# A sum over groups of heads, split by halves of the heads: one half beside the last attention, the other beside the output projection

## The reference

```python
    alpha = jax.nn.softmax(jnp.stack(lses, axis=0), axis=0)
    o = jnp.sum(alpha[..., None] * jnp.stack(outs, axis=0), axis=0)
    y = o.reshape(B, S, DIL_WIDTH).astype(h.dtype) * jax.nn.silu(gate)
    return y @ w_out
```

## Time and profile before

| what | value |
|---|---|
| median of 3 runs | 2482.21 us |
| lowest and highest run | 2479.74, 2485.02 us |
| the profiled execution's own time | 2479.8 us |
| its span in the trace | 2478.0 us |
| PE busy | 2193.9 us, 89% of the span |
| DVE, ACT, POOL busy | 953.9, 873.6, 865.2 us |

### The profile page before, as it was taken

The page is one execution under the profiler, slowest core; times in us unless marked ns, Lnnn a source line. Parts: engine busy times, 40 slices in busy tenths (PEclk is TensorE's granted clock), DMA queues, the critical chain, the costliest instruction groups (busy, mean ns, idle before and its releaser), DMA issues. The chain is left out here.

```text
span 2478.0 us, 26013 instructions
## 1 busy us (share of the span) xinstructions
PE 2193.9 (89%) x10048; PEld 1736.3 (70%) x10048; DVE 953.9 (38%) x1603; ACT 873.6 (35%) x1740; POOL 865.2 (35%) x454
## 2 busy tenths in 40 slices
PE   4998999999957997857999999887987998999998
PEld 3877788888846775646677777675765456887876
DVE  1333334633453356553253411247552642210121
ACT  2544445655353554323232122231322222321231
POOL 3422233333314322244344433342224313444442
PEclk9999999999978999978999999898998998999999
DMA  4312122222332211222352233232223432332321
GB/s 154 100 53 69 52 84 71 86 86 81 129 110 75 90 52 58 70 85 85 102 149 89 86 86 94 73 102 69 81 79 124 131 113 66 96 103 85 102 90 64
DMA packets 130634, 221.32 MB, mean 89 GB/s; under 512 B 8744, under 2 KB 58456, under 8 KB 130304
## 3 DMA queue, kind: packets, MB, share of 16 engines
q1 hardware_dynamic: 110720, 168.63, 22.5%
q0 software_dynamic: 9104, 32.66, 4.0%
q10 hardware_dynamic: 10688, 18.35, 2.1%
HBM read 199.40 MB, written 19.62 MB: 88 GB/s over the span
## 5 line engine op out<-in xcount | busy, mean ns | idle before, releaser
L2238 POOL TENSOR_TENSOR lo_ring<-raw_ring,hi_ring 128x1024 fp32r<-128x1024 f32 (+1 forms) x304 | 732.0, 2430 | 1188.3 <-ACT hi_ring L1891 1188.2
L855 PE MATMUL bank<-xh,hi_ring 128*128 128x512 f32 x1472 | 601.7, 409 | 5.4 <-DVE xl L1337 3.3
L855 PE MATMUL bank<-xh,lo_ring 128*128 128x512 f32 x1472 | 582.4, 396 | 0.0
L855 PE MATMUL bank<-xl,hi_ring 128*128 128x512 f32 x1472 | 581.6, 395 | 0.0
L1891 ACT CAST hi_ring<-raw_ring 128x1024 fp32r<-128x1024 f32 (+1 forms) x304 | 303.4, 1046 | 512.9 <-PE bank L855 491.2
L855 PEld LDWEIGHTS bank<-xh,hi_ring 128*128 128x128 f32 x1472 | 282.5, 192 | 77.2 <-issue 18.5
L855 PEld LDWEIGHTS bank<-xh,lo_ring 128*128 128x128 f32 x1472 | 281.0, 191 | 61.5
L855 PEld LDWEIGHTS bank<-xl,hi_ring 128*128 128x128 f32 x1472 | 282.5, 192 | 57.8 <-issue 2.6
L855 PE MATMUL bank<-hi_ring,xh 128*128 128x512 f32 (+1 forms) x608 | 249.8, 411 | 11.4 <-POOL lo_ring L2238 6.4
L855 PE MATMUL bank<-hi_ring,xl 128*128 128x512 f32 (+1 forms) x608 | 242.2, 398 | 0.0
L855 PE MATMUL bank<-lo_ring,xh 128*128 128x512 f32 (+1 forms) x608 | 242.2, 398 | 0.0
(11 more groups left out here) (246 smaller groups left out, 2477.7 us busy)
## 6 DMA issues: line engine op xcount, KB each, us to landing
raw_ring<-in_ffn_w_in SPq DMA_DIRECT2D x176, 256.0 KB, 3.1
raw_ring<-in_dil_w_in SPq DMA_DIRECT2D x80, 512.0 KB, 3.7
raw_ring<-in_ffn_w_out SPq DMA_DIRECT2D x44, 512.0 KB, 3.8
raw_ring<-in_diff_w_in SPq DMA_DIRECT2D x32, 512.0 KB, 3.7
raw_ring<-in_w_in SPq DMA_DIRECT2D x32, 512.0 KB, 3.7
arena<-scratch_heads POOLq DMA_DIRECT2D x4, 1584.0 KB, 13.9
scratch_gates<-arena ACTq DMA_DIRECT2D x24, 256.0 KB, 2.1
arena<-scratch_gates POOLq DMA_DIRECT2D x24, 256.0 KB, 3.8
```

Source lines behind the costliest of these rows:

```text
L855: ins = T.matmul(bank[pb][:, 0:S if p.form == "feature" else p.cols], lhsT, rhs, start=(k == 0 and m == 0), stop=(k == p.K - 1 and m == le ...
L2238: G.tensor_tensor(lo, raw_ring[:, p % RAW, 0:q.kq * q.n], hi.bitcast(F32), ALU.subtract).then_inc(lowered, 1)
```

## The change

The three groups are summed by halves of 8 heads. Half 0 (units 0, 2, 4) is done beside the gate panels, while unit 5's attention still runs: one job of it to a mac. For this unit 4's attention is placed more densely (`LAST_RATIO` 1.1), the first two tiles of half 0 are loaded by POOL ahead of the gate panels, and tiles 2 and 3 by ACT, once the tile that held their place is summed. Half 1 is loaded by POOL after unit 5's store. After the gate panels half 0 is turned (4 transposes a tile, one bank), rounded, and its four remainders are made before any work of half 1. The first output panel begins with the 4 chunks of half 0; its second step for tile n waits for the turned half 1 of tile n (`late`), and half 1's jobs stand between its macs. ACT now scales 12 of the 24 slices of a half tile (4 of group 1 and 8 of group 2), DVE 12. The barrier ahead of the output panels is gone; waits on `mixed` take its place where the outputs are written over the gate. The norm row has a place of its own and is loaded after unit 5's store.

```diff
-ACT_HEADS = 12
+SCALED = 4
+HALF_ROW = 8 * ROW
...
-UNIT_RATIO, GATE_RATIO, FIRST_HEADS = 0.85, 2.5, 14
+UNIT_RATIO, LAST_RATIO, GATE_RATIO = 0.85, 1.1, 2.5
...
-        interleave(projections(u), side, UNIT_RATIO)
+        interleave(projections(u), side, LAST_RATIO if u == 5 else UNIT_RATIO)
...
-    def first_heads():
-        plan.job("mix_load")
-        for _ in range(FIRST_HEADS):
+    def first_half():
+
+        for n in range(2):
+            plan.job("mix_load", 0, n)
+        for step in range(16):
             yield
-        plan.job("mix_ratio", 0)
-        plan.job("mix_weight", 0)
-        plan.job("mix_scale", 0)
-
-    interleave(gate_panels(plan, w, 9 * D, 0), chain(side, first_heads()), GATE_RATIO)
+            if step % 3 == 2 and step < 12:
+                plan.job("mix_ratio", 0, step // 3)
+            elif step % 3 == 0 and 0 < step < 13:
+                n = step // 3 - 1
+                plan.job("mix_weight", 0, n)
+                plan.job("mix_scale", 0, n)
+            elif step % 3 == 1 and 1 < step < 14:
+                n = step // 3 - 1
+                plan.job("mix_sum", 0, n)
+            if step in (9, 10, 13, 14):
+                plan.job("mix_gate", 0, (9, 10, 13, 14).index(step))
+
+    def last_store():
+        plan.job("row", "post0")
+        for n in range(NT):
+            plan.job("mix_load", 1, n)
+        yield
+
+    side, beside = chain(side, last_store()), first_half()
+    owed = 0.0
+    next(beside)
+    for _ in gate_panels(plan, w, 9 * D, 0):
+        owed += GATE_RATIO
+        while owed >= 1.0:
+            owed -= 1.0
+            next(side, None)
+        next(beside, None)
+    run_all(side)
+
+    use = [plan.job("mix_turn", 0, n, banks=(4 + n,)) for n in range(NT)]
     for n in range(NT):
+        plan.job("mix_lower", 0, n)
+    plan.job("mix_ratio", 1, 0)
+    plan.job("mix_weight", 1, 0)
+    plan.job("mix_scale", 1, 0)
+    plan.job("mix_ratio", 1, 1)
+    plan.job("mix_sum", 1, 0)
+    plan.job("mix_weight", 1, 1)
+    plan.parts = tuple(((f"drained{4 + n}", use[n][0]),) for n in range(NT))
+    late = [(), (), (), ()]
+    main = plan.panel("y", "dil_w_out", 0, 512, "tile", at=(0,), late=late)
+    for _ in range(4):
+        next(main)
+    for n in range(NT):
+        plan.job("mix_gate", 1, n)
+        use = plan.job("mix_turn", 1, n, banks=(4 + n,))
+        late[n] = ((f"drained{4 + n}", use[0]),)
         if n + 1 < NT:
-            plan.job("mix_ratio", n + 1)
-        plan.job("mix_sum", n)
-        if n + 1 < NT:
-            plan.job("mix_weight", n + 1)
-        plan.tile_parts("mix", n)
-        if n + 1 < NT:
-            plan.job("mix_scale", n + 1)
-        if n:
-            plan.job("lower", n - 1)
-    plan.job("lower", NT - 1)
+            plan.job("mix_scale", 1, n + 1)
+            if n + 2 < NT:
+                plan.job("mix_ratio", 1, n + 2)
+            plan.job("mix_sum", 1, n + 1)
+            if n + 2 < NT:
+                plan.job("mix_weight", 1, n + 2)
+        plan.job("mix_lower", 1, n)
+        next(main)
+    run_all(main)
+    plan.parts = ((), (), (), ())
...
+        late_heads = [arena[:, a:a + 3 * HALF_ROW].rearrange("p (g c) -> p g c", g=3) for a in (v_at + NT * 512, after_rope, after_rope + 3 * HALF_ROW, 3 * 4 * S)]
+        heads = [[arena[:, a:a + 3 * HALF_ROW].rearrange("p (g c) -> p g c", g=3) for a in (rope_at, v_at, rope_at, v_at)], late_heads]
+        mix = [[arena[:, stage_at + 512 * n:stage_at + 512 * n + 512] for n in range(NT)], [arena[:, 4 * S + 512 * n:4 * S + 512 * n + 512] for n in range(NT)]]
...
+        def load_half(engine, half, n):
+            src = scratch[:, n * P:(n + 1) * P, half * HALF_ROW:(half + 1) * HALF_ROW]
+            engine.dma_start(heads[half][n], src.rearrange("g p c -> p g c")).then_inc(heads_landed[half][n], 16)
...
+                else:
+                    for name_value in p.late[b]:
                        T.wait_ge(*ready_value(name_value))
...
-                elif kind == "mix":
+                elif kind == "mix_turn":
+                    half, n = a
                     T.wait_ge(mixed, job.n + 1)
-                    turn_tile(job, mix[:, a[0] % 2, :], a[0])
+                    empty(4 + n, job.use[0])
+                    for k in range(4):
+                        ins = T.transpose(tile(bank[4 + n], k), tile(mix[half][n], k), ident)
+                    ins.then_inc(filled[4 + n], 1)
...
+                    if p.w == "dil_w_out":
+                        V.wait_ge(mixed, NT + o + 1)
...
+            def mix_scale(m, half, n):
+                H, i = heads_of(half, n), m % 2
+                V.wait_ge(weights_made, m + 1)
+                for g, k in ((0, 8), (1, SCALED)):
+                    w = corr[i][:, g * 8:g * 8 + k].unsqueeze(2).to_broadcast([P, k, HD])
                     V.tensor_tensor(H[:, g, 0:k, 0:HD], H[:, g, 0:k, 0:HD], w, ALU.mult).then_inc(heads_scaled, 1)
 
...
+            def mix_sum(m, half, n):
+                H = heads_of(half, n)
+                o_ = mix[half][n].rearrange("p (h r) -> p h r", h=8)
+                V.wait_ge(heads_scaled, 2 * m + 2)
+                V.wait_ge(slices_scaled, m + 1)
+                if half == 0 and n == 0:
+                    V.wait_ge(stored[0], 16 * (1 + 1 + 4))
+                V.tensor_tensor(o_, H[:, 0, :, 0:HD], H[:, 1, :, 0:HD], ALU.add).then_inc(v_step, own.up())
                 V.wait_ge(v_step, own.n)
+                V.tensor_tensor(o_, o_, H[:, 2, :, 0:HD], ALU.add).then_inc(heads_mixed, 1)
+
+            def mix_gate_half(m, half, n):
+                V.wait_ge(heads_mixed, m + 1)
+                V.wait_ge(drained[n], gate_panel[0, half].use[n])
+                V.scalar_tensor_tensor(mix[half][n], mix[half][n], 0.5, tile_gate(n, half), ALU.mult, ALU.mult).then_inc(mixed, 1)
+
+            def mix_lower(half, n):
+                b, cols = 4 + n, slice(n * P, (n + 1) * P)
+                tiles_rounded.up()
+                V.wait_ge(x_rounded, tiles_rounded.n)
+                V.tensor_tensor(xl[:, 4 * half:4 * half + 4, cols], bank[b][:, :].rearrange("p (a b) -> p a b", a=4),
+                                xh[:, 4 * half:4 * half + 4, cols].bitcast(F32), ALU.subtract).then_inc(drained[b], 1)
 
...
-                    n = a[0]
-                    A.wait_ge(corr_made, n + 1)
-                    A.activation(corr[n % 2], corr[n % 2], ACT.Exp).then_inc(corr_exped, 1)
+                    A.wait_ge(corr_made, job.n + 1)
+                    A.activation(corr[job.n % 2], corr[job.n % 2], ACT.Exp).then_inc(corr_exped, 1)
+                    if 1 <= job.n <= 2:
+                        A.wait_ge(heads_mixed, job.n)
+                        load_half(A, 0, job.n + 1)
                 elif kind == "mix_weight":
-                    n = a[0]
-                    A.wait_ge(weights_made, n + 1)
-                    for g, h in [(1, h) for h in range(ACT_HEADS, DIL_HEADS)] + [(2, h) for h in range(DIL_HEADS)]:
-                        o_ = heads[:, n, g, h * ROW:h * ROW + HD]
-                        ins = A.activation(o_, o_, ACT.Copy, scale=corr[n % 2][:, 16 * g + h:16 * g + h + 1])
-                    ins.then_inc(third_weighed, 1)
-                elif kind in ("norm_tile", "mix", "o_tile"):
+                    half, n = a
+                    A.wait_ge(weights_made, job.n + 1)
+                    for g, h in [(1, h) for h in range(SCALED, 8)] + [(2, h) for h in range(8)]:
+                        o_ = heads[half][n][:, g, h * ROW:h * ROW + HD]
+                        ins = A.activation(o_, o_, ACT.Copy, scale=corr[job.n % 2][:, 8 * g + h:8 * g + h + 1])
+                    ins.then_inc(slices_scaled, 1)
+                elif kind == "mix_turn":
+                    half, n = a
+                    A.wait_ge(filled[4 + n], job.use[0])
+                    A.copy(xh[:, 4 * half:4 * half + 4, n * P:(n + 1) * P], bank[4 + n][:, :].rearrange("p (a b) -> p a b", a=4)).then_inc(x_rounded, tiles_rounded.up())
+                elif kind in ("norm_tile", "o_tile"):
...
+                    if a[0] == "post0":
+                        G.wait_ge(stored[1], 16 * (1 + 1 + 4))
...
-                    for buf in range(2):
-                        G.wait_ge(stored[buf], 16 * (1 + 1 + 4))
-                    for n in range(NT):
-                        G.dma_start(heads[:, n], scratch[:, n * P:(n + 1) * P, :].rearrange("g p c -> p g c")).then_inc(heads_landed[n], 16)
+                    half, n = a
+                    if half == 0:
+                        G.wait_ge(stored[0], 16 * (1 + 1 + 4))
+                        G.wait_ge(stored[1], 16 * (1 + 1))
+                        if n == 0:
+                            G.wait_ge(filled[6], use_of["v_turn", plan.count["v_turn"] - 1][0])
+                    elif n == 0:
+                        G.wait_ge(stored[1], 16 * (1 + 1 + 4))
+                    load_half(G, half, n)
                 elif kind == "lambda":
```

96 lines of the change are left out of this document (41 added, 55 removed).

## The result

| what | before | after |
|---|---|---|
| median, highest and lowest of 6 runs each | 2483.61 us (2479.4 to 2488.34) | 2493.8 us (2489.96 to 2499.99) |
| the span of the profiled execution | 2478.0 us | 2495.7 us |

The ratio is 1.0045, 95% interval 1.0026 to 1.0064: slower, by about 11 us. I had predicted 2482.0 us and a range of 2471 to 2491.

A forecast was written before the change was run, and what follows sets the result against it. The tensor engine, busy 89% of the span, was taken as the bound, so only its idle or slow-clock time could be won. Terms -0.5 + 6.0 - 5.7 = -0.2 us on a 2482.21 us median gave 2482.0 us, range 2471 to 2491.

The forecast's parts named there:

- Part 1: Unit 5's stretch with ratio 1.1: the last attention but one placed in 19 steps instead of 24; -0.5 us (-1.6 to +2).
- Part 2: Half 0 beside the gate panels: list order delays the last attention 5.0 us, loads +0.3, clock +0.7; +6.0 us.
- Part 3: From the last gate matmul to the last output matmul: 76.3 us instead of 82.05; -5.7 us (-11.8 to -1).
- E: End of the last gate matmul, 681.15 us in the kernel before; forecast near 687 after the change.
- The ring: Serial chain between the late output steps, as each output tile's product precedes the next gate half on VectorE's list; 17.0 us.
- late steps: The first output panel's second steps, each waiting for half 1 of its tile; forecast to run partly at the lower clock.
- Z: End of the last output matmul; forecast at E + 76.3, near 763 us.
- wrong: Signs against: gate panels' end moves under 2 or over 9 us, clock stays 1.0 in the ring, half 1's transposes await loads.
- right: Signs for: gate-stage waits of 5 to 7 us, first output matmul about 3 us after E, paired pauses between later steps.
- B: Rival, faster: the clock stays up or the attention's pauses are shorter; 2476 or 2473 us; chance 0.33.
- C: Rival, slower: the attention's ring passes on two tiles' work in full, 13.8 instead of 5.0 us; 2490.8 us; chance 0.24.
- A: The forecast itself: the tensor engine's idle hole is halved, but attention delay and lower clock cancel it; -5 to +5 us; 0.43.

The follow-up runs named there:

- e4_ratio: Changed kernel with `LAST_RATIO` back from 1.1 to 0.85, so unit 4's attention is placed as before; 2494.69 us, 1.0041 of the kernel before.
- e3_few_slices: Changed kernel with ScalarE scaling one slice instead of 12 for tiles 0 and 1 of half 0; 2483.36 us, 1.0008 of the kernel before.
- e6_late: Changed kernel with half 1's list reordered, first four output steps listed earlier, half 0's slices moved behind the last attention; 2484.71 us, 1.0010 of before.
- e1_short_rest: Changed kernel with GpSimd's remainders of the first layer's weight pieces cut from 1024 to 32 columns; 2485.84 us, 1.0010 of the kernel before.
- e12_placed_short: e8_placed with GpSimd's remainders of the output weights cut to their first 32 columns; 2467.12 us, 0.9936 of the kernel before.
- e8_placed: Changed kernel with half 1's list reordered, first output steps earlier, half 0's jobs hand-placed, ScalarE scaling 8 slices; 2469.49 us, 0.9945 of before.

## Why the prediction was wrong

**Part 1 (-0.5)**: worth nothing. Unit 5's stretch is 66.17 us where it was 66.16, and e4_ratio has the same time.

**Part 2 (+6.0, measured +8.1)**: the mechanism was right, link by link. Slices at 642.36, cast, tanh, mask 5, exp 5, turn late; then the last value product. e3_few_slices and e6_late take the waits away whole, and 6.7 of the 8.1 us. The added pauses were 3.5 us and not 5.0. What was mis-sized is the clock, put at +0.7: the same matmuls took 4.6 us longer. After a wait of only 1.66 us the level was 1.2 GHz for 6.6 us, and again after the 3.00. I had priced a single pause of 4.2 us.

**Part 3 (-5.7, measured +2.6)** is the step that failed, by 8.3 us, and the reason for the miss. Its terms, measured from E: the first output step at 7.4 instead of 3.1 (+4.3); the four first steps in 12.9 us instead of 10.9 (+2.0, the level was 1.2 GHz from 697.3 to 704.1, after the wait of 3.95); the pause behind them 4.86 us, about as predicted, so that the first late step stands at 25.7 instead of 19.4. That this pause agreed is in part luck: two 128x24 products are held in it (1.15 us at 714.45 and 1.79 at 716.09), and in e1_short_rest it is 4.01. The ring itself was predicted at 17.0 us and is 16.8 (7.1, 5.2 and 4.5). The late steps took 5.5, 4.7, 4.9 and 5.0 us (the last is 750.40 to 777.47, less 22.1 for the second panel) instead of 4.6 and three of 4.4 (+2.2).

So the statement "at E VectorE still has tile 3's sum, two gate halves ... the first lower starts at E + 2.4" was the false one: the sum started at E + 2.9 and the remainders at E + 6.6. The hold of 3.9 us at 686.84 is most of that. With GpSimd's remainders left out (e1_short_rest) the remainders of half 0 start at E + 2.0, the first late step at E + 18.4, and Z is at E + 77.2 instead of 84.6: 7.4 of the 8.3 us. What is left is within 1 us of the prediction, but by terms that cancel: in that run the late steps take 3.2 us more than I had, the ring 1.3 less, and the first late step stands 1.0 earlier. I counted VectorE's work in the gate stage by its durations in a stretch where GpSimd was still, and put it beside GpSimd's remainders. How long GpSimd works at a time stood in the earlier trace rows, 4.75 us for two pieces. The kernel before also shows the hold itself, in a layer that I did not read: its L1465 take up to 2.63 us (above), those beside a remainder of GpSimd. VectorE's two-input instructions took 4.13, 2.74 and 4.77 us beside such remainders against 0.2 and 0.69 elsewhere, the neighbours with one input or one from a bank 0.18 and 0.62, and the same instruction 0.20 once the remainders are left out (e12_placed_short). The Trainium skill has the rule, in SBUF — State Buffer, section "Who interferes with whom": a VectorE instruction with two SBUF inputs contends with a GpSimd instruction that reads SBUF; its section "SBUF: two separate sides" says that the one that starts first has the ports for the whole instruction. By the first these traces agree. By the second the instruction of e8_placed would have gone on at the next boundary, after 2.4 us; it waited for two remainders, 4.77. Others were let in at the first boundary (last section). I had not weighed the rule.

The late steps were slow, each of them, and so were the turn and the first steps behind E. The rule of the Trainium skill that I had set against this part (TensorE: Matmul & The Clock Gate, section "HAM oscillation — how this bites in real kernels") agrees with these rows; I had given it the late steps and nothing else.

Of the signs, those of "wrong" told little: the clock did not stay at 1.0, no transposes of half 1 waited for loads, and the gate stage grew by 8.1 us, inside the 2 to 9 (E as the trace reads is 11.7 us later, 3.6 of it from ahead of the gate panels). The sign that told was one of "right" that failed, the first output matmul 7.4 us after E instead of 3. Two numbers of the working are slips that change nothing: 4.89 / 20 is 0.2445, and 19.4 and a step of 2.7 make 22.1, not 22.3.

**Rivals**: B asked for a clock that stays up, which it did not. C had its end (slower) right but not its place: the attention's ring passed on 3.5 us, not 13.8, and the rest of the loss came from the clock in it and from behind E. A's hole was not halved: its idle time fell from 29.7 to 23.3 us, 6.4 less; the 9.0 us by which the matmuls there became slower took it back, as did those in the gate stage.
